# Dividing all five tiles of probabilities on GpSimd in a two-layer streaming encoder

## What is computed

```python
logits = jnp.where(mask, logits + decay, NEG)
p = jax.nn.softmax(logits, axis=-1).astype(v.dtype)
return jnp.einsum('bhqk,bkhd->bqhd', p, v)
```

## Time and profile before

| | us |
|---|---|
| median of 3 runs | 1712.37 |
| lowest and highest | 1711.02, 1714.63 |
| the profiled execution's own time | 1713.24 |
| its span, first to last instruction | 1711.4 |
| PE busy | 1597.2 (93%) |
| DVE busy | 879.3 (51%) |
| ACT busy | 673.9 (39%) |
| POOL busy | 137.7 (8%) |

### The profile page before, as it was taken

How to read it: one execution, slowest core, us unless ns; L and a number is a source line. 1 busy time by engine, 2 the same in 40 slices (tenths; PEclk the granted TensorE clock), 3 DMA queues, 4 the chain that set the end, 5 groups by cost and what they waited for, 6 DMA issues and landing times.

```text
span 1711.4 us, 29076 instructions
## 1 busy us (share of the span) xinstructions
PE 1597.2 (93%) x11188; PEld 1506.0 (88%) x11188; DVE 879.3 (51%) x1554; ACT 673.9 (39%) x1198; POOL 137.7 (8%) x167
## 2 busy tenths in 40 slices
PE   4999979998999999999988897999899999999994
PEld 3777768888999999999978686888899999999994
DVE  4222058884444444454485246888444544444545
ACT  3212148874333322323223435877433223223213
POOL 2110011110100000000030001111010000000003
PEclk8999969999999999999989898999999999999997
DMA  7245232202221221212200536220222222212001
GB/s 252 90 135 177 98 88 63 67 11 99 74 99 50 98 80 67 98 54 82 75 28 8 197 129 191 77 77 2 99 75 99 66 82 98 78 69 98 25 0 56
DMA packets 119308, 145.99 MB, mean 85 GB/s; under 512 B 17632, under 2 KB 95520, under 8 KB 119248
## 3 DMA queue, kind: packets, MB, share of 16 engines
q1 hardware_dynamic: 119248, 145.16, 25.9%
HBM read 120.54 MB, written 24.60 MB: 85 GB/s over the span
## 4 chain that ended last, share of the span: by engine, by line
PE 79%; DVE 8%; issue 5%; ACT 4%; DMA 2%; POOL 1%; SPq 0%; DVEq 0%; POOLq 0%; ACTq 0%
PE ps L1365 72%; DVE nmx L1080 2%; DVE ptl L1105 2%; PE ps L1527 2%; ACT pth L796 1%; PE ps L1571 1%; PE ps L1573 1%; PE ps L1572 1%; PE ps L1542 1%; DVE ol L1116 1%; POOL sacc L609 1%; DVE prob L1094 1%; ACT oh L807 0%; DVE acc L1220 0%; ACT wh L702 0%
## 5 line engine op out<-in xcount | busy, mean ns | idle before, releaser
L1220 DVE TENSOR_TENSOR acc<-acc,ps 128x592 f32<-128x592 f32 (+1 forms) x256 | 194.9, 762 | 305.5 <-PE ps L1365 304.0
L702 ACT ACTIVATE wh<-raw 128x2048 fp32r<-128x2048 f32 (+1 forms) x90 | 167.4, 1876 | 249.1 <-PE ps L1365 249.1
L1365 PE MATMUL ps<-hh,wh 128*128 128x296 f32 (+1 forms) x1024 | 224.3, 300 | 13.9 <-DVE acc L1220 11.4
L980 DVE TENSOR_TENSOR wl<-raw,wh 128x2048 fp32r<-128x2048 f32 (+1 forms) x90 | 198.5, 2243 | 74.2 <-ACT wh L702 74.2
L1365 PE MATMUL ps<-hl,wh 128*128 128x296 f32 (+1 forms) x1024 | 222.2, 298 | 0.0
L1365 PE MATMUL ps<-hh,wl 128*128 128x296 f32 (+1 forms) x1024 | 221.8, 298 | 0.0
L1365 PE MATMUL ps<-xgh,wh 128*128 128x296 f32 (+1 forms) x1024 | 221.5, 297 | 0.0
L1365 PE MATMUL ps<-xgl,wh 128*128 128x296 f32 (+1 forms) x1024 | 221.2, 297 | 0.0
L1365 PE MATMUL ps<-xgh,wl 128*128 128x296 f32 (+1 forms) x1024 | 220.2, 296 | 0.0
L1365 PEld LDWEIGHTS ps<-hh,wh 128*128 128x128 f32 x1024 | 166.3, 190 | 16.5 <-DVE acc L1220 13.7
L1365 PEld LDWEIGHTS ps<-hl,wh 128*128 128x128 f32 x1024 | 167.4, 190 | 0.0
(11 more groups left out here) (197 smaller groups left out, 2788.6 us busy)
## 6 DMA issues: line engine op xcount, KB each, us to landing
raw<-in_w_up SPq DMA_DIRECT2D x32, 1024.0 KB, 5.6
raw<-in_w_down SPq DMA_DIRECT2D x32, 1024.0 KB, 7.0
raw<-in_w_in_a SPq DMA_DIRECT2D x12, 1024.0 KB, 7.3
kv_mla<-stn SPq DMA_DIRECT2D x24, 256.0 KB, 2.1
raw<-in_w_o_a SPq DMA_DIRECT2D x4, 1024.0 KB, 7.0
natk<-kv_mla SPq DMA_DIRECT2D x8, 512.0 KB, 4.3
raw<-in_w_o_b SPq DMA_DIRECT2D x4, 1024.0 KB, 11.0
q_mla<-stn SPq DMA_DIRECT2D x16, 192.0 KB, 1.9
```

Of the source, the lines that this page charges most:

```text
L702: s.activation(wh[:, j % 4, 0:r * c], raw[:, j % 4, 0:r * c], ACT.Copy).then_inc(hi_done, 1)
L980: v.tensor_tensor(wl[:, j % 4, 0:r * c], raw[:, j % 4, 0:r * c], wh[:, j % 4, 0:r * c].bitcast(F32), ALU.subtract).then_inc(lo_done, 1)
L1220: v.tensor_tensor(a, a, two_banks(2 + m % 2, n), ALU.add).then_inc(acc_done, 1)
L1365: return te.matmul(out, a, b, start=start, stop=stop)
```

## The change

All five divisions of a head go to POOL. It does them as a two-input product: one input is the tile, the other the column of reciprocals, spread over all columns of the tile with a step of zero. `split_v` is cut into three parts. In every second head of the loop the parts stand behind the products of tiles 0, 1 and 2; the first two pairs of values are split in front of all products. ACT's `scale3` and DVE's `scale` are gone, and so is `p3_ready`: PE waits on `p_ready` for every tile.

```diff
+            def normalise(layer, h, c, u):
+                n = unit_keys(u)[1]
+                rows = P if u < NT else TX
+                off = P_OFF[u] + (64 if u < NT else 0)
+                pool.wait_ge(recip_done, h * 5 + (5 * HEADS * layer + u + 1))
+                g.tensor_tensor(prob[0:rows, c, off:off + n], prob[0:rows, c, off:off + n],
+                                rs[0:rows, u:u + 1].to_broadcast([rows, n]), ALU.mult).then_inc(p_ready, 1)
...
-            def split_v(layer, j, slot, turn, after_av=False):
+            def split_v(layer, j, slot, turn, part, after_av=False):
...
+                if part == 0:
...
+                    pool.wait_ge(v_hi, j * 3 + 3 + 3 * PAIRS * layer)
+                    return
+                for src, r, t in (views[0:1] + views[2:3] if part == 1 else views[1:2]):
                     i = g.tensor_tensor(vl[r, slot, t, :].rearrange("p t (h d) -> p t h d", h=2), src,
                                         vh[r, slot, t, :].bitcast(F32).rearrange("p t (h d) -> p t h d", h=2), ALU.subtract)
...
+                def head(h, c):
+                    for u in range(5):
+                        normalise(layer, h, c, u)
+
+                def head_and_v(h, c, j, slot, turn):
+                    for u in range(3):
+                        normalise(layer, h, c, u)
+                        split_v(layer, j, slot, turn, u, True)
+                    normalise(layer, h, c, 3)
+                    normalise(layer, h, c, 4)
+
+                for j in range(2):
+                    for part in range(3):
+                        split_v(layer, j, j, 0, part)
+                for h in range(4):
+                    head(h, h % 2)
+                with pool.Fori(0, PAIRS // 2 - 1) as i:
+                    head_and_v(4 * i + 4, 0, 2 * i + 2, 0, i + 1)
+                    head(4 * i + 5, 1)
+                    head_and_v(4 * i + 6, 0, 2 * i + 3, 1, i + 1)
+                    head(4 * i + 7, 1)
...
-                        if u == 0 and not first:
-                            scale3(h - 1, 1 - c)
...
-                        scale(h - 1, 1 - c, 4)
                         turned(h, 1)
...
-                    scale(h, c, 0)
                     if not first:
                         turned(h, 2)
...
                     row_max(h, 3)
-                    scale(h, c, 1)
                     if not first:
                         turned(h, 3)
...
-                    scale(h, c, 2)
                     recip(h, 3)
...
-                    if u == 3:
-                        pe.wait_ge(p3_ready, h + H0)
-                    else:
-                        pe.wait_ge(p_ready, h * 4 + (4 * H0 + [-3, -2, -1, 0, 0][u]))
+                    pe.wait_ge(p_ready, h * 5 + (U0 + u - 4))
```

More of the change, by code:

```diff
@@ L633, in _ @@
                               tab[0:TILE_ROWS[t], t, 8 * hf:8 * hf + 8, :]).then_inc(aug_done, 1)
-            def split_v(layer, j, slot, turn, after_av=False):
-                if layer == 0:
-                    pool.wait_ge(nat_v, j * 64 + 64)
-                else:
-                    pool.wait_ge(nat_qk[slot], turn * 80 + (80 + 40 * PAIRS))
-                if after_av:
-                    pool.wait_ge(av_done, j * 2 + (HEADS * layer - 2))
+            def normalise(layer, h, c, u):
[7 more added lines that the diff above has]
+                if part == 0:
+                    if layer == 0:
+                        pool.wait_ge(nat_v, j * 64 + 64)
+                    else:
+                        pool.wait_ge(nat_qk[slot], turn * 80 + (80 + 40 * PAIRS))
+                    if after_av:
+                        pool.wait_ge(av_done, j * 2 + (HEADS * layer - 2))
                 views = []
@@ L655, in split_v @@
-                pool.wait_ge(v_hi, j * 3 + 3 + 3 * PAIRS * layer)
-                for n, (src, r, t) in enumerate(views):
+                if part == 0:
+                    src, r, t = views[0]
+                    g.tensor_tensor(vh[r, slot, NT, :].rearrange("p (h d) -> p h d", h=2), src.rearrange("p t h d -> p (t h) d"),
+                                    ones[r, :].rearrange("p (h d) -> p h d", h=2), ALU.mult).then_inc(v_hi, 1)
+                    for src, r, t in views[1:]:
+                        g.tensor_copy(vh[r, slot, t, :].rearrange("p t (h d) -> p t h d", h=2), src).then_inc(v_hi, 1)
+                    pool.wait_ge(v_hi, j * 3 + 3 + 3 * PAIRS * layer)
+                    return
@@ L657, in split_v @@
+                for src, r, t in (views[0:1] + views[2:3] if part == 1 else views[1:2]):
                     i = g.tensor_tensor(vl[r, slot, t, :].rearrange("p t (h d) -> p t h d", h=2), src,
                                         vh[r, slot, t, :].bitcast(F32).rearrange("p t (h d) -> p t h d", h=2), ALU.subtract)
[L659 to L665, removed]
+                if part == 2:
+                    i.then_inc(v_split, 1)
@@ new lines, in attention @@
+            def attention(layer):
+                def head(h, c):
[17 more added lines that the diff above has]
+                    head(4 * i + 7, 1)
@@ L667, in mlp_finish @@
+            attention(0)
             def mlp_finish(layer):
@@ L680, in _ @@
                 g.tensor_tensor(rc[:, i, :], ss[:, i, :], mhalf[:], ALU.pow).then_inc(zr_ready, 1)
[L681 to L685, removed]
+            attention(1)
             sum_squares(3)
@@ L1086, in recip @@
                     v.reciprocal(rs[0:rows, u:u + 1], sm[0:rows, u:u + 1]).then_inc(recip_done, 1)
-                def scale(h, c, u):
-                    n = unit_keys(u)[1]
-                    rows = P if u < NT else TX
-                    off = P_OFF[u] + (64 if u < NT else 0)
-                    dve.wait_ge(recip_done, h * 5 + (U0 + u + 1))
-                    v.tensor_scalar(prob[0:rows, c, off:off + n], prob[0:rows, c, off:off + n], rs[0:rows, u:u + 1],
-                                    None, ALU.mult).then_inc(p_ready, 1)
                 def group(h, q, what):
```

14 lines of the change are left out of this document (removed).

## The result

The kernel after took 1700.28 us in the median of 5 runs (1698.39 to 1703.42), the kernel before 1712.37 (1709.66 to 1714.64) beside it. The ratio is 0.9931, 95% interval 0.9914 to 0.9948: a gain of 12.1 us, between 9 and 15. The profiled execution took 1700.21 us, its span is 1698.4.

What follows compares the result with a forecast made beforehand. In attention a chain between ACT and DVE sets the pace, with one of five divisions on the path. Steps -7.5 and start +1.0 gave -6.5 us: 1705.9 against the median of 1712.37, range 1702.0 to 1711.5.

Steps and rivals of the forecast that it cites:

- the 0.27: DVE's division of tile 1 delays the remainder of tile 3, and so PE, by 0.27 us a head, 14 times a layer.
- the sum: Both attention stages: -7.5 us from the steps and +1.0 from the start of layer 0, together -6.5 us.
- The other four divisions: Tiles 0, 2 and 4 on DVE and tile 3 on ACT: taking them away gains nothing.
- POOL's price: POOL's product at 2.12 ns a column and 0.19 us fixed, 4.5 us a head for five products.
- spare time: Each POOL product is done before PE wants it; tightest at tile 3 of a head with values, 1.9 us.
- the threshold: Rival, 0.07: a spread operand at 4.2 ns a column or more fills POOL at 19.8 us a pair; at 5 ns, 1749.
- The start of layer 0: POOL splits both first pairs of values before any product, PE waits about 1.6 us: +1.0 us, ends 0.6 and 3.0.
- the steps: The 0.27 us got 28 times in the attention of both layers: -7.5 us.
- the half that I took: Start of layer 0: each us at half clock was taken to cost half a us.
- The larger gain: Rival, 0.07: PE follows at its own 317.92, 28 x 0.39 less 0.6: 1702.1 us.
- the start costs more: Rival, 0.10: at the start the clock rises much later, or the steps give less; gain 3 us, 1709.5.
- the port: Rival, 0.05: POOL's product of tile 1 blocks DVE for 0.77 us; 0.5 net a head, 14 us slower, 1726.

Runs made afterwards that it cites:

- the starts filled: Kernel after plus products nobody reads on PE in its idle time ahead of each attention (33 and 22): 1705.15 us, ratio 0.9971.
- the doubled and tripled products: Kernel after with each POOL product done twice, 1705.63 us, or three times, 1804.53 us, the extra ones into an unused buffer.
- filled kernel: Unread products on PE ahead of each attention, in some also in five more idle places; with all places, 1702.11 us on after, 1705.48 on before.

## Why the prediction was wrong

**What bounds the kernel, and the 0.27.** Right: 5.03 us unchanged, 0.27 off the other half, steps of 9.69 and 9.93 for a forecast of 9.7 and 9.9, PE 0.14 behind the remainder. The cause is shown by moving tile 1 alone and by moving the other four without it. The size, 14 x 0.27 = 3.8 us a layer, is best seen in layer 1: 3.8 to 3.9 in every pair of profiles. That the two layers gave 7.52 in the first pair, the 7.5 of the sum to the digit, is partly luck, since attention of layer 0 alone took 174.6 and 172.9 in two executions of before.

**The other four divisions.** Right: nothing.

**POOL's price and spare time.** The price was too high by a fifth (4.5 against 3.73 us a head), on the safe side; the spare time was right, and no run contradicts the threshold. Neither touched the sum.

**The start of layer 0.** The mechanism was right: PE waits for POOL, 2.3 us and not 1.6, since the load came 1.1 us later (POOL began on it at 233.88 instead of 232.81). The price of +1.0 is neither confirmed nor refuted. The first pair of profiles shows 0.04 (3.78 - 3.74), beside a low stretch that was 3.4 us shorter, but the second profile of before has a shorter one still (20.5 us) without the change. In the means of the profiles layer 0 gained 1.2 us less than layer 1, and it took 0.7 longer than in the two profiles of the kernel that moves tile 1 alone and keeps the start. With stages that differ by 1.4 to 1.7 us between executions of one kernel, anything from 0 to about 1.5 fits. With the starts filled the same wait costs about 4 us.

**The sum.** This is the step that failed. I added terms for the stages of the change and put the rest of the kernel at nothing, without a reason: no term, and no room of its own in the range, for the time outside attention and for what differs between executions. Even without the start's term the sum gives 1704.9; the remaining 4.6 us to 1700.28 lie there. What the runs showed in its place: in the first pair of profiles 5.5 us in untouched stages, beside 95 and 70 us of low clock in them, and up to 5 us between profiles of one kernel there (1360.3 and 1365.2 us outside attention in after). With all executions pooled, 9.3 (standard error 0.7) remain of the 12.1, so 2.8 of the 12.1 were the luck of five runs. Of the 9.3, the steps explain 7.5, or 6.5 together with a start of +1.0, and 1.8 to 2.8 stay. At an equal mean granted clock (a line of time on clock through all executions of six kernels, common slope, 0.001 of clock for 0.8 us) before and after differ by 8.1, and the granted clock accounts for 1.2. Whether what stays belongs to the shorter steps or to chance is open: doing tile 1 twice gave +8.2 (standard error 1.3), which decides nothing. A range with 3 us more on both sides for stages that the change doesn't touch would have held the result.

The same line bears on a price inside the sum. 0.001 of mean clock is 3.4 us at the lower level, so a low us costs some 0.24 us of kernel time, an estimate from these runs. In attention of layer 0 the two profiles of before differ by 1.7 us beside 5.8 us of low clock, 0.3 a us. Both lie below the half that I took, as an estimate, for a clock that rises later.

**The rivals.** None came true. The larger gain (1702.1, by PE following at its own 317.92) comes close in size for the wrong reason: PE still starts 0.14 behind the remainder. That the start costs more is what the kernels with filled starts bring out. What one rival calls the port shows in no step of the runs: with POOL busy for 17.89 us a pair DVE is busy for the same 15.68.

## What to carry to other kernels

- Find the one instruction on the path and move that; here one of five divisions carried the whole gain, and the move of the other four is free only as long as the receiving engine has room, which the doubled and tripled products bound (17.9 us of 19.6 a pair is free, 26.1 is not).
- A difference between two profiled executions in code that is the same is no gain of the change: profile the same kernel twice before explaining it, and give a forecast room for it.
- What stands behind a wait for a load must not stand ahead of what another engine wants next; and an engine that is made faster ahead of such a place turns its gain into a wait there (PE's wait of 2.29 us became 5.66), so mend the order first and the clock second.
- Work that is put into an engine's idle time must fit what is left of it where the engine reaches that work, not the whole of it: 22 products sized by 6.82 us of idle time began 4.01 us into it and delayed the stage by 3 to 4 us.

## What the hardware showed that I had not expected

- POOL's two-input product takes 1.67 ns a column when one input is a column spread with a step of zero, 2.15 with a plain block (1066 and 1317 ns at 528 columns).
- POOL busy 91% of a pair left DVE's and ACT's busy time as it was (15.68 and 15.04 us).
- The same idle stretch of PE is followed by the lower clock in one execution and not in another (1.88 us idle in the stretch ahead of 1300 in both profiles of before, then a granted clock of 0.66 and of 1.00); executions of one kernel spread over more than 10 us (1704.1 to 1718.8 for before), and over those of before the time falls as the mean granted clock rises from 0.960 to 0.973.
- Keeping PE's clock up with unread products took the low clock from between 100 and 134 us down to between 59 and 70, and was worth 7 us in the kernel before, none in the kernel after until the wait for the load was out of the way. Every filled kernel pays 3 to 4 us of its gain for the products ahead of layer 1.
- A us of low clock went with some 0.24 us of kernel time between executions (0.8 us for 0.001 of mean clock, 3.4 us at the lower level).
